# Third-branch gate tiles of the first block as pairs of seven half-size products

## What is computed

```python
h = rmsnorm(x, norm_mix_pre[l])
proj = h @ w_in[l]
(q, k, v, g_ret, sc_b, sc_c, sc_x, cf_a, cf_b, gate_logits) = split(proj)
...
y_ret = (silu(g_ret) * o) @ w_ret_out[l]
y_sc = (sc_b * u) @ w_sc_out[l]
y_cf = c @ w_cf_out[l]
gates = sigmoid(gate_logits).reshape(B, S, 3, 1024)
merged = gates[:, :, 0] * y_ret + gates[:, :, 1] * y_sc + gates[:, :, 2] * y_cf
x = x + rmsnorm(merged @ w_o[l], norm_mix_post[l])
```

## Time and profile before

| | |
|---|---|
| median of 3 runs | 3080.21 us (3079.84 to 3081.51) |
| the profiled execution | 3080.47 us, of it the span 3079.2 us |
| PE busy | 3070.0 us |
| DVE busy | 2029.2 us |
| ACT busy | 1400.2 us |
| POOL busy | 619.4 us |
| granted clock of PE | 1.00 of full speed |

### The profile page before, as it was taken

One profiled execution on the slowest core, in us unless ns is written; L12 is line 12 of the kernel. 1 busy time (PEld: TensorE's weight loads), 2 busy tenths in 40 slices (PEclk: granted clock), 3 DMA queues, 4 the chain that ended last, 5 costly groups with the idle time before them and its releaser, 6 DMA issues.

```text
span 3079.2 us, 40010 instructions
## 1 busy us (share of the span) xinstructions
PE 3070.0 (100%) x15812; PEld 2624.5 (85%) x15812; DVE 2029.2 (66%) x2728; ACT 1400.2 (45%) x2197; POOL 619.4 (20%) x514
## 2 busy tenths in 40 slices
PE   9999999999999999999999999999999999999999
PEld 8888888888888888888888889988888888998887
DVE  6876456667787655666768766657656765755864
ACT  4333334335433333443555544536645554444752
POOL 1202212341121121234213301120011420211001
PEclk9999999999999999999999999999999999999999
DMA  4684546556667454555664464657552254564443
GB/s 172 217 238 163 141 165 189 170 154 216 202 205 226 174 148 151 192 178 164 187 204 172 123 202 141 183 161 182 160 185 98 81 157 155 174 176 126 134 131 133
DMA packets 153962, 517.92 MB, mean 168 GB/s; under 512 B 17680, under 2 KB 17936, under 8 KB 143312
## 3 DMA queue, kind: packets, MB, share of 16 engines
q1 hardware_dynamic: 139040, 419.18, 40.2%
q0 software_dynamic: 13440, 91.46, 14.0%
q10 hardware_dynamic: 1296, 4.72, 0.5%
HBM read 488.55 MB, written 140.51 MB: 204 GB/s over the span
## 4 chain that ended last, share of the span: by engine, by line
PE 97%; DVE 2%; ACT 1%; DMA 0%; SPq 0%; issue 0%; POOL 0%; DVEq 0%; POOLq 0%
PE ps L682 95%; PE ps L776 1%; PE ps L1138 1%; DVE r L1934 0%; DVE f L1939 0%; DVE wl L1924 0%; DMA raw<-wsum 0%; DVE f L2002 0%; SPq L2964 0%; DMA X<-x_in 0%; ACT wh L1258 0%; PE ps L726 0%; DVE f L2070 0%; ACT L1295 0%; DVE f L2276 0%
## 5 line engine op out<-in xcount | busy, mean ns | idle before, releaser
L682 PE MATMUL ps<-h,wh 128*128 128x512 f32 (+1 forms) x5568 | 1521.5, 360 | 0.4 <-DVE wl L1924 0.2
L682 PEld LDWEIGHTS ps<-h,wh 128*128 128x128 f32 x5568 | 993.4, 188 | 162.3 <-issue 2.6
L682 PE MATMUL ps<-h,wl 128*128 128x512 f32 (+1 forms) x2784 | 1000.4, 359 | 0.0
L1924 DVE TENSOR_TENSOR wl<-raw,wh 128x1024 fp32r<-128x1024 f32 (+2 forms) x655 | 787.2, 1211 | 263.1 <-ACT wh L1258 259.3
L1258 ACT CAST wh<-raw 128x1024 fp32r<-128x1024 f32 (+2 forms) x668 | 645.1, 981 | 425.9 <-PE ps L682 402.1
L682 PEld LDWEIGHTS ps<-h,wl 128*128 128x128 f32 x2784 | 522.7, 188 | 78.7
L682 PE MATMUL ps<-r,wh 128*128 128x512 f32 x1536 | 474.5, 390 | 1.0 <-DVE r L1934 0.6
L682 PEld LDWEIGHTS ps<-r,wh 128*128 128x128 f32 x1536 | 284.9, 188 | 59.1 <-issue 2.2
L682 PE MATMUL ps<-r,wl 128*128 128x512 f32 x792 | 304.3, 389 | 0.0
L1355 ACT CAST r<-f 128x512 fp32r<-128x512 f32 (+1 forms) x194 | 114.5, 596 | 401.4 <-DVE f L2374 169.0
L2841 POOL TENSOR_TENSOR f<-f,f 128x512 f32<-128x512 f32 x64 | 107.2, 1675 | 670.3 <-DVE f L2188 670.3
(11 more groups left out here) (218 smaller groups left out, 3161.5 us busy)
## 6 DMA issues: line engine op xcount, KB each, us to landing
raw<-wst SPq DMA_DIRECT2D x376, 512.0 KB, 4.2
raw<-wsum SPq DMA_DIRECT2D x120, 512.0 KB, 4.2
raw<-wpr SPq DMA_DIRECT2D x74, 512.0 KB, 3.9
wsum<-wpr POOLq DMA_DIRECT2D x31, 1024.0 KB, 8.9
wsum<-wsum POOLq DMA_DIRECT2D x62, 512.0 KB, 5.9
raw<-wst SPq DMA_DIRECT2D x48, 320.0 KB, 3.2
raw<-wpr SPq DMA_DIRECT2D x38, 256.0 KB, 3.0
r<-r SPq DMA_DIRECT2D x64, 128.0 KB, 2.3
```

Source lines behind the costliest of these rows:

```text
L682: return e.matmul(o, a, b, start=start, stop=stop, skip_group_check=True)
L1924: e.tensor_tensor(l[:, 0:WIDTH[c]], source(c), h[:, 0:WIDTH[c]].bitcast(F32), ALU.subtract).then_inc(*lo_cut.up(("lo", c)))
```

## The change

In layers 0 and 1 the eight gate tiles of the third branch (b = 2) are made as four pairs by `two_tiles`, as the second block's are. For this, per layer:

- PE: 4 pairs x 7 products x 12 matmuls of 128x256 (336) take the place of 8 x 24 matmuls of 128x512 (192); the output products stand between them.
- POOL makes the four combinations of h near the start of `mixer1`: 1, 6 and 4 ahead of the rotary products, 3 behind them.
- ACT and DVE get `mixed_hi` and `mixed_lo` behind ca2/cb2 (1), ca3/cb3 (6), k0 (4) and in g0 (3), and the copies and additions of `two_gates` and `four_parts` in the gate stage.
- Eight more blocks of weights (four a layer) are copied and summed in DRAM: blocks are copied also beside q, k and v in layer 0, and POOL has more `sum_slot` places.
- The rows are saved before `mix` in layer 1 and brought back in both layers; in layer 0 they come from `x_in`.
- `ones` lies elsewhere and is written once a layer.

```diff
+SINGLE = {0: 8, 1: 8, 2: 0}
...
+GATE_AT = (62, 63, 64, 65, 60, 61, 66, 67)
...
         def gate_free(L, b, j):
 
+            if L < 2 and j >= SINGLE[b]:
+                return (("cf_lo", L, 3), ("cf_lo", L, 3), ("gated", L, 1, 5), ("gated", L, 1, 7))[j // 2]
...
+                for j in range(SINGLE[b], 8, 2):
+                    slot(f"{L}/gate{g}_{j}*0")
+                    two_tiles(L, f"{L}/gate{g}_{j}", lambda i: some(j + (i > 0), (range(4), range(2), range(2, 4))[i]))
...
+                for j in range(SINGLE[b], 8, 2):
+                    c = NAME[f"{L}/gate{b}_{j}*0"]
+                    cut(c + 3)
+                    two_gates(L, b, j, lambda: cut(c + 4), lambda: cut(c + 5), lambda i: cut(c + 6 + i))
...
+                    if j > 1:
+                        mixed_hi(L, "16"[j - 2])
...
+                    if r == 1:
+                        mixed_hi(L, "4")
...
                     if h == 0:
                         query_key(1)
+                        mixed_hi(L, "3")
...
+            def mixed_lo(L, m):
+                lo_part(mixed("3", int(m == "3"), F32), mixed(m, 0), mixed(m, 1), at("mixed_hi", L, m), ("mixed_lo", L, m))
...
                 w.wait_ge(*at("root", "y", B, t))
-                if B > 4 or B in FFN:
-                    w.wait_ge(*at("landed", f"back{B}{t}" if B in FFN else f"back{B}"))
+                w.wait_ge(*at("landed", f"back{B}{t}" if B in FFN else f"back{B}"))
...
+                w.wait_ge(*at("done", (f"{LAYER[B]}/gate{'c' if B > 4 else 2}_6", "c21")))
+                e.dma_start(X[:, 0:8 * S], x_in if B == 1 else kept_x).then_inc(*landed(f"back{B}"))
...
                 step(A, A, h_quarter(1, 0, 1), ALU.add, ("mixed", L, "4"), seen("4", 0))
+                more()
                 step(A, h_quarter(1, 0, 0), h_quarter(1, 1, 0), ALU.subtract, ("mix", L, "3", 0), at("mixed_lo", L, "4"))
...
-                for _ in range(4 if L else 0):
-                    sum_slot()
-                for r in range(4):
-                    roped(L, r, 52)
+                def all_roped():
+                    for r in range(4):
+                        roped(L, r, 52)
+
+                if L:
+                    save_rows(2)
+                mix(L, 2 * L, all_roped)
                 for h in range(4):
                     small_step("ret_stats", L, h)
-                for _ in range(8):
+                for _ in range(14):
                     sum_slot()
```

More of the change, by code:

```diff
@@ L95, in plan @@
         for b, w in enumerate(("w_ret_out", "w_sc_out", "w_cf_out")):
-            one(f"gate{b}_", D1["gate"] + 1024 * b, 0)
+            if SINGLE[b]:
+                one(f"gate{b}_", D1["gate"] + 1024 * b, 0)
             for j in range(8):
-                if j < 7:
+                if j < SINGLE[b] - 1:
                     one(f"gate{b}_", D1["gate"] + 1024 * b, j + 1)
                 if j % 2 == 0:
+                    if j >= SINGLE[b]:
+                        two_tiles(f"{l}/gate{b}_{j}", A, l, *(D1["gate"] + 1024 * b + (j + i) * P for i in range(2)))
                     out.append((f"{l}/pr{b}_{j}",
@@ L889, in gate_proj, with some @@
                 n = AHEAD[b]
-                for j in range(n):
+                for j in range(min(n, SINGLE[b])):
                     tile(f"{L}/gate{g}_{j}", xs)
-                for j in range(8):
-                    if j + n < 8:
-                        tile(f"{L}/gate{g}_{j + n}", xs)
+                def some(j, ks):
                     key = ("pr", L, b, j)
@@ L899, in gate_proj @@
                     h, l = weights(name)
-                    o = take(key)
-                    for k in range(4):
+                    o = bank(key) if ks[0] else take(key)
+                    for k in ks:
                         w.wait_ge(*at(*ready, k))
-                    last = group(o, h, l, [(j % 2 * 4 + k) * P for k in range(4)], ys)
-                    closes = (("closed", NAME[name]),) if j % 2 else ()
-                    last.then_inc(*group_done.up(("done", key), *closes))
+                    last = group(o, h, l, [(j % 2 * 4 + k) * P for k in ks], [ys[k] for k in ks], ks[0] == 0, ks[-1] == 3)
+                    if ks[-1] == 3:
+                        closes = (("closed", NAME[name]),) if j % 2 else ()
+                        last.then_inc(*group_done.up(("done", key), *closes))
+                for j in range(SINGLE[b]):
+                    if j + n < SINGLE[b]:
+                        tile(f"{L}/gate{g}_{j + n}", xs)
+                    some(j, range(4))
+                for j in range(SINGLE[b], 8, 2):
+                    slot(f"{L}/gate{g}_{j}*0")
+                    two_tiles(L, f"{L}/gate{g}_{j}", lambda i: some(j + (i > 0), (range(4), range(2), range(2, 4))[i]))
             def product(key, name, what, xs, start=False, stop=False):
@@ L1289, in small_step @@
                     acc, hi, _ = SUM_AT["ln"]
+                    if not second:
+                        w.wait_ge(*at("done", ("o", L, 3)))
+                        ones(L)
                     hi_part(F(acc), R(hi), at("ln_added", L, 3) if second else at("ln_sum", L), ("ln_hi" + second, L))
@@ L1453, in gate_proj @@
             def gate_proj(L, b, cut_merged=None):
-                for j in range(AHEAD[b]):
+                for j in range(min(AHEAD[b], SINGLE[b])):
                     slot(f"{L}/gate{b}_{j}")
-                for j in range(8):
-                    if j + AHEAD[b] < 8:
+                for j in range(SINGLE[b]):
+                    if j + AHEAD[b] < SINGLE[b]:
                         slot(f"{L}/gate{b}_{j + AHEAD[b]}")
@@ L1897, in scalar @@
             w.wait_ge(*at("landed", "cst"))
-            ones(1)
             for L in (0, 1):
@@ L2199, in gate_proj @@
                     gated(L, b, j)
+                for j in range(SINGLE[b], 8, 2):
+                    c = NAME[f"{L}/gate{b}_{j}*0"]
+                    cut(c + 3)
+                    four_parts(f"{L}/gate{b}_{j}", gate_at(L, b, j), gate_at(L, b, j + 1), lambda: cut(c + 4), lambda: cut(c + 5))
+                    cut(c + 6)
+                    gated(L, b, j)
+                    cut(c + 7)
+                    gated(L, b, j + 1)
                     if cut_merged and j:
+                        cut_merged(j - 2)
                         cut_merged(j - 1)
                 if cut_merged:
+                    cut_merged(6)
                     cut_merged(7)
+            def mixed_lo(L, m):
+                lo_part(mixed("3", int(m == "3"), F32), mixed(m, 0), mixed(m, 1), at("mixed_hi", L, m), ("mixed_lo", L, m))
             def four_parts(name, g0, g1, first, second):
@@ L2285, in mixer1 @@
                         *dve_tile.up(("glu", L, j), ("free", key)))
-                for nm, j in (("q", 0), ("k", 0), ("q", 1), ("k", 1)):
+                    if j > 1:
+                        mixed_lo(L, "16"[j - 2])
+                for r, (nm, j) in enumerate((("q", 0), ("k", 0), ("q", 1), ("k", 1))):
                     slot(f"{L}/{nm}{j}")
+                    if r == 1:
+                        mixed_lo(L, "4")
                 def query_key(p):
@@ L2321, in mixer1 @@
                         query_key(1)
+                        mixed_lo(L, "3")
                     w.wait_ge(*at("g_gate", L, h))
@@ L2472, in heads @@
                     if h in MIXED_AT:
[L2473 to L2474 removed]
+                        mixed_lo(L, MIXED_AT[h])
                 def scores(h):
@@ L2753, in boundary @@
             def boundary(B):
-                if B > 4:
+                if B not in FFN:
                     rows_back(B)
                 gains(B)
+                for _ in range(2 if B in FFN else 0):
+                    sum_slot()
                 roots(B, ("y", 0), ("y", 1))
```

49 lines of the change are left out of this document (26 added, 23 removed).

## The result

The changed kernel takes **3107.14 us** (median of four runs, 3105.89 to 3109.28), the kernel before 3080.74 in the same session: a ratio of 1.0087, 95% interval 1.0069 to 1.0104, or 26.4 us more. The forecast was 3089, its range 3074 to 3093. The sign was right and the size was not: the result lies 14 us above the upper end.

What follows compares the result with a forecast made beforehand. PE's own work and waits were taken to bound the kernel. 3080.5 us, less 7.4 for eight pairs, plus 8.0 of lateness in each of two layers, less 0.3 for the median, gave 3089 us; range 3074 to 3093.

Steps and rivals of the forecast that it cites:

- step 5: Before the first retention, PE waits for combination 3 and the decayed scores: 8.0 us late in all per layer, 6.6 to 9.5.
- What PE saves: Third branch's gate tiles: a pair takes 9.95 us instead of 10.88, so eight pairs save 7.4 us.
- What the gate stage adds: Gate stage: added chunks, partial-product copies, additions, returned rows, block copies and sums cost PE 0.
- Steps 1 to 3: Mixer start: DVE's new splits 3.5 us plus collisions 8.2, less idle time 5.3, make `query_key(0)` late by 6 us.
- Rival B: Mixer start: POOL's work finds gaps, only combination 3 comes 0.6 us late a layer; 3074.0 down to 3072.8 us, chance 0.12.
- rival C: Mixer start: half of the collisions happen, lag 2.3 us, 2.9 to 5 us a layer; 3078.6 to 3083 us, chance 0.32.
- Step 4: Before the scores of head 0, PE waits 4.7 us: a lag of 6 less a margin of 1.3.
- up to 0.5 each more, and DVE reaches the `mixed_lo` later: Combination 3's six instructions, if they too take turns with taps: 9.5 us late per layer, the upper end.
- step 2: Before `query_key(0)`, all eight POOL instructions of combinations 6 and 4 meet a tap, 1.03 us each: 8.2 us.
- Layer 1 has the same: Layer 1's mixer start: same order and spacing as layer 0, with combination 1 later, so 8.0 us too.
- Rival D: Layer 0 at 40 to 104 us: extra block copies make transfers land late, 3 us more; above 3092 us, chance 0.06.

Runs made afterwards that it cites:

- experiment 1: The changed kernel with the third branch's gate tiles single again, the combinations still made early: 3114.50 us.
- experiment 8: The changed kernel with one ScalarE activation put back at the start, so that its table is loaded ahead of the first products: 3106.90 us.
- experiment 7: The changed kernel with unread matmuls in PE's two waits of layers 0 and 1, and ten block sums instead of 14 ahead of the layer norm: 3102.62 us.
- experiment 9: Experiment 5 with no block sum between the last rotary sum and first retention statistic, and combination 3 split two gate tiles later: 3091.81 us.
- experiment 12: Experiment 9 with the combinations one step earlier, split behind sc tiles 0 to 3, and two sums back in layer 0's feed-forward block: 3088.41 us.
- experiment 14: The changed kernel with combinations moved to the layer norm and second gate branch, the early activation back, block sums reordered: 3080.21 us.
- experiment 2: The changed kernel with combinations 1, 6, 4 behind sc tiles 1, 2, 3, combination 3 behind the first gate tile, the early activation back: 3113.82 us.
- experiment 3: The changed kernel with combination 3 alone moved behind sc tile 1: 3115.65 us.
- experiment 5: Experiment 2 with the block sums in GpSimd's queue reordered, so that four no longer stand between combinations 4 and 3: 3101.64 us.
- experiment 4: The changed kernel with unread matmuls in PE's two waits of layers 0 and 1, 16 before head 0's scores, 24 before the first retention: 3106.12 us.

## Why the prediction was wrong

The measured time lies 18 us above the forecast. Two steps failed: the second wait (step 5), which left out what combination 3 does to DVE, and the clock behind that wait, which was not in the sum. The mechanism, DVE's lag at the start of the mixer, is the one that the runs show.

**What PE saves: right.** -7.4 us forecast, 7.4 between experiment 1 and the change, 3.8 and 3.6 in the landmarks. The estimate from the gap formula of the Trainium skill (TensorE: Matmul & The Clock Gate, "Back-to-back issue gap") was 9.5; the runs bear out the rows. The pair's pitch after, sums at 384.13 and 399.63, is 15.5 us; 15.4 was forecast.

**What the gate stage adds: right at 0.** No wait of PE over 0.1 us stands between the turn of head 3 and the boundary in either layer.

**Steps 1 to 3, lag of 6 us: right but for the table load.** `query_key(0)` begins at 107.78 instead of 100.43, 7.35 us later; experiment 8 takes 1.2 of it away. Eight collisions cost 7.6 us (8.2 forecast). Rival B and rival C fall: all eight met a tap.

**Step 4, first wait of 4.7: right in kind.** 4.07 us, and the scores 5.4 us late in all.

**Step 5, second wait, "8.0 in all, 6.6 to 9.5": failed in size, on the path over DVE.** The retention is 11.4 us late. The last rotary product ends at 112.9 instead of 111.6, which is the table load. Combination 3 takes 10.6 us (112.84 to 123.47) where I took 8.1 from layer 2, where DVE is quiet: all six of its instructions met taps or splits. I had summed GpSimd, then ScalarE, then DVE. But ScalarE had rounded combination 3 at 124.55, and DVE, without a pause since 107.78, came to its `mixed_lo` only at 125.48. What ended last was DVE's own list. From `query_key(0)` to the decayed scores it took 19.44 us (107.78 to 127.22) instead of 12.08 (100.43 to 112.51): 1.15 for the `mixed_lo` and 6.2 for six collisions. With the lag of 7.35 that is 14.7 us, of which the 3.3 that the decayed scores had been ahead of PE take up a part, and 11.4 are left. The sentence on this, "up to 0.5 each more, and DVE reaches the `mixed_lo` later", named it, but put it into the upper end and not into the number, and priced it by GpSimd's 0.5 each, not by the 1.03 each that it costs DVE; the case in which all collide was the case of step 2 too, and should have been used in both.

**Missing from the sum: the clock.** Every term had PE resume at full speed. Behind the second wait it did not: 2.9 and 2.5 us, together 5.4, shown by the windows and by experiment 7. No row of before has a wait of this length with work behind it (the longest is 1.06 us, at the start), so the price could not be read; what PE does after such a wait was one more unknown that should have widened the range.

**"Layer 1 has the same": failed.** It lost 15.5 us, 1.2 more than layer 0 though it has no table load. The rows are saved first, so combination 1 is made from 831.86 to 842.34 and meets taps and splits as well: DVE's first five taps there take 6.49 us instead of 3.39, and `query_key(0)` is 8.9 us late against the layer's start, not 7.35. A wait of 2.20 us stands at 874.37, where DVE has just split the weights, at 873.05, behind four taps that took 6.85 us beside combination 4. Step 4 had put late weight chunks at 0 to 0.5 us.

**Step by step:** 16 us forecast for two layers, 29.8 measured (14.3 + 15.5). Of the 13.8 between, 5.4 is the clock behind the second wait and 1.2 the table. The rest, 7.2, is what is left over, 2.2 in layer 0 and 5.0 in layer 1: combination 3 beside DVE in both layers and combination 1 in layer 1. How it divides between them was not measured. Then -7.4, and 0.3 + 2.7 + 1.8 - 1.8 in the feed-forward blocks and the later layers, which gives the 25.4 us between the spans. Of the 2.7, 2.4 are one wait (at 1524.22) beside the two block sums that the change adds at the end of layer 1's feed-forward block, and it is gone in experiments 9, 12 and 14, which have none there. Rival D, late transfers at 40 to 104 us, did not happen: the spread's transfers were issued 7.35 us late and no more, and landed in 2.3 us as before. The queues did matter elsewhere, by their order (experiments 2, 3 and 5).

## What to carry to other kernels

Work of two engines that take turns is priced by where it stands, not by its size: beside the same 20 additions a layer PE lost 14.3 and 15.5 us at the start of the mixer and little 200 us later. (Experiment 14 also has the table load back and its block sums in another order; the table load was 1.2 us of the loss, and what the order alone gives was not run.) So look for the stretch in which neither engine has a deadline, and check when the first consumer wants the result. When a term of the sum rests on a collision in one step, use it in every later step that the same engines share. Behind a new wait of PE add its slow clock, here 2.5 to 2.9 us for waits of 3.4 and 4.2. And look at what stands behind moved work in every in-order queue, block sums and table loads too.

## What the runs showed of the hardware

- PE's granted clock fell to half behind waits of 3.4 and 4.2 us and cost 2.9 and 2.5 us there. It also fell behind one of 2.20 us (0.68 in the window from 875 to 880). Useless products in a wait kept it at full (experiments 4 and 7).
- Seven additions of GpSimd that read SBUF held taps and a split of DVE up by 0.96 us each; seven memsets did not hold them up. One split beside three additions in a row lost 1.29 for each (experiment 12). Memsets of 128x512 took 0.48 us each beside DVE's taps (four in 1.93 us), additions 1.7 to 1.9.
- One accumulating transfer of 1 MB beside sixteen of 128 KB raised their time to land from 2.3 to 6.5 us.
- The same table load ran at 25.69, ahead of its sigmoid's wait for PE, with `ones(1)` in ScalarE's list, and at 35.99, behind that wait, without it (experiment 8: 25.68 again). Taking a harmless activation away so moved 1.28 us onto the path.
